# A hybrid attention layer on one core: a shorter lead, POOL's products moved to DVE, and the FFN's first groups in another order

## What is computed

```
h    = rmsnorm(x, pre_mix_norm)
proj = h @ w_in                                  # 1024 x 3072
rq, rk, rv, rg, mq, mk, mv = split(proj)
ret  = silu(rg) * head_rmsnorm(retention(rotary(rq), rotary(rk) / 8, rv))     # 4 heads
moba = causal softmax attention(mq, mk, mv) with a T5 bucket bias             # 8 heads of 64
mix  = concat([ret, moba]) @ w_out
x    = x + rmsnorm(mix, post_mix_norm)
h    = rmsnorm(x, pre_ffn_norm)
f    = (silu(h @ w_gate) * (h @ w_up)) @ w_down
x    = x + rmsnorm(f, post_ffn_norm)
```

## Time and profile before

| | |
|---|---|
| median of 3 timed runs | 317.04 us (316.82 to 317.07) |
| profiled execution | 318.91 us, its span 317.1 us |
| PE busy | 305.3 us (96%) |
| DVE, ACT, POOL busy | 182.7, 153.3, 27.6 us |
| granted PE clock | 0.998 of full speed |
| read from memory | 57.10 MB, 183 GB/s over the span |

### The profile page before, as it was taken

How to read it: one execution, slowest core, us unless ns; L and a number is a source line. 1 busy time by engine, 2 the same in 40 slices (tenths; PEclk the granted TensorE clock), 3 DMA queues, 4 the chain that set the end, 5 groups by cost and what they waited for, 6 DMA issues and landing times.

```text
span 317.1 us, 4124 instructions
## 1 busy us (share of the span) xinstructions
PE 305.3 (96%) x1432; PEld 248.8 (78%) x1432; DVE 182.7 (58%) x255; ACT 153.3 (48%) x254; POOL 27.6 (9%) x31
## 2 busy tenths in 40 slices
PE   7999987999999999999999999999999999999992
PEld 3788866888888888768888888888888888888881
DVE  2858265697467487899555555544444454551426
ACT  4889626446608174676444444444433333340322
POOL 4021056000002000540000000000000000000001
PEclk9999999999999999999999999999999999999999
DMA  6999974314541543169965555555566565400003
GB/s 216 398 407 373 413 308 134 134 66 153 180 144 57 198 156 111 66 231 317 367 203 179 179 190 180 168 184 191 198 198 198 198 196 183 149 0 0 0 2 132
DMA packets 17517, 58.35 MB, mean 184 GB/s; under 512 B 1997, under 2 KB 2517, under 8 KB 17504
## 3 DMA queue, kind: packets, MB, share of 16 engines
q1 hardware_dynamic: 17136, 57.06, 51.6%
q0 software_dynamic: 368, 1.11, 1.0%
HBM read 57.10 MB, written 1.06 MB: 183 GB/s over the span
## 4 chain that ended last, share of the span: by engine, by line
PE 85%; DVE 7%; ACT 3%; DMA 2%; POOL 2%; issue 1%; SPq 0%; DVEq 0%
PE bank L951 25%; PE bank L953 24%; PE bank L952 24%; PE bank L961 4%; DVE w_lo L681 2%; DMA raw<-in_w_in 2%; PE bank L978 1%; POOL xs L437 1%; PE bank L982 1%; PE bank L986 1%; ACT w_hi L451 1%; DVE d_lo L876 1%; ACT kz L518 1%; PE bank L1049 1%; DVE res L942 1%
## 5 line engine op out<-in xcount | busy, mean ns | idle before, releaser
L951 PE MATMUL bank<-w_hi,a_hi 128*128 128x512 f32 x256 | 101.9, 398 | 0.0
L953 PE MATMUL bank<-w_hi,a_lo 128*128 128x512 f32 x256 | 100.1, 391 | 0.0
L952 PE MATMUL bank<-w_lo,a_hi 128*128 128x512 f32 x256 | 99.6, 389 | 0.0
L617 ACT ACTIVATE sil<-bank,rstd 128x256 f32<-128x256 f32 x22 | 10.4, 473 | 96.1 <-PE bank L953 93.7
L953 PEld LDWEIGHTS bank<-w_hi,a_lo 128*128 128x128 f32 x256 | 48.0, 188 | 10.6
L952 PEld LDWEIGHTS bank<-w_lo,a_hi 128*128 128x128 f32 x256 | 48.2, 188 | 9.8
L951 PEld LDWEIGHTS bank<-w_hi,a_hi 128*128 128x128 f32 x256 | 48.1, 188 | 9.4
L869 DVE TENSOR_TENSOR w_lo<-raw,w_hi 128x1024 fp32r<-128x1024 f32 x40 | 49.6, 1276 | 6.7 <-ACT w_hi L602 6.7
L681 DVE TENSOR_TENSOR w_lo<-raw,w_hi 128x1024 fp32r<-128x1024 f32 x32 | 42.2, 1345 | 19.4 <-ACT w_hi L451 19.4
L884 DVE SCALAR_TENSOR_TENSOR hid<-bank,rstd,sil 128x256 f32<-128x256 f32 x22 | 10.7, 485 | 73.9 <-ACT sil L617 73.9
L602 ACT ACTIVATE w_hi<-raw 128x1024 fp32r<-128x1024 f32 x40 | 40.5, 1057 | 0.5 <-DMA raw<-in_w_gu 0.5
(11 more groups left out here) (119 smaller groups left out, 307.5 us busy)
## 6 DMA issues: line engine op xcount, KB each, us to landing
raw<-in_w_gu SPq DMA_DIRECT2D x44, 512.0 KB, 4.3
raw<-in_w_dn SPq DMA_DIRECT2D x22, 512.0 KB, 4.6
raw<-in_w_in SPq DMA_DIRECT2D x20, 512.0 KB, 8.5
raw<-in_w_out SPq DMA_DIRECT2D x8, 512.0 KB, 3.2
raw<-in_w_in SPq DMA_DIRECT2D x8, 256.0 KB, 5.8
xs<-in_x SPq DMA_DIRECT2D x2, 512.0 KB, 8.6
bias<-bias_row POOLq DMA_DIRECT2D x1, 1024.0 KB, 10.2
out<-res SPq DMA_DIRECT2D x4, 256.0 KB, 2.0
```

The lines of the kernel that those rows point to most:

```text
L617: act.activation(sil[:, t, :], pg[:, t, 0:FG], ACT.Silu, scale=rstd[:, X1_, t:t + 1]).then_inc(sil_ready[t], 1)
L951: pe.matmul(acc, hi, wh, start=first, stop=False)
L952: pe.matmul(acc, hi, wl, start=False, stop=False)
L953: return pe.matmul(acc, lo, wh, start=False, stop=last)
```

## The change

- LEAD is 4. ACT's evacuations of q, k and v stand ahead of the `w_hi` of their round. `LO_UNITS`, which says which `w_lo` DVE does in rounds 16 to 19, is shifted by one unit.
- The warm-up matmuls read a constant tile of ones; DVE's memset is gone. The bias row product stands behind the first block of unit 0; ACT issues the DMAs of its inputs, before its first table load.
- K's heads with odd numbers are copied out of PSUM by DVE, before the `w_lo` of unit 13, instead of by ACT.
- The three 128x1024 products of POOL are done by DVE: two in round 22, one behind the `w_lo` of `w_out`. POOL's memsets of `rqz` no longer wait for them. The residual of tile 1 goes to DVE as well; that of tile 0 stays.
- In the FFN each group does both tiles of gate and up first, then the down product of the group before for tile 0, then turns both tiles of `hid`, then the down product for tile 1. Group 0 and 1 are apart: group 1's gate and up go to bank45, and group 0's `hid` is turned, into bank01, in the middle of group 1's second tile. ACT and DVE have their queues rearranged to match.

```diff
-LEAD = 5
-LO_UNITS = {16: [], 17: [21], 18: [22], 19: [23, 24]}
+LEAD = 4
+LO_UNITS = {16: [], 17: [20], 18: [21], 19: [22, 23]}
...
-        pg = bank01
-        pt = bank45
+        def pg(g):
+            return bank45 if isinstance(g, int) and g == 1 else bank01
+        def pt(g):
+            return bank01 if isinstance(g, int) and g == 0 else bank45
...
-            pool.dma_start(rel[0:BUCKETS, :], rel_bias).then_inc(rel_loaded, 16)
-            pool.dma_start(bucket[:, :], bucket_c).then_inc(rel_loaded, 16)
...
-            for t in range(NT):
-                pool.wait_ge(x_loaded[t], 16)
-                pool.tensor_tensor(xg[:, t, :], xs[:, t, :], gp[:, :], ALU.mult).then_inc(xg_ready, 1)
-            pool.wait_ge(xg_ready, NT)
-            pool.tensor_tensor(gp[:, :], gm[:, :], gp[:, :], ALU.mult).then_inc(xg_ready, 1)
             pool.wait_ge(k_turned, NT)
-            pool.wait_ge(xg_ready, NT + 1)
+            pool.wait_ge(rstd_ready, NT)
...
+            act.dma_start(bucket[:, :], bucket_c).then_inc(rel_loaded, 16)
+            act.dma_start(rel[0:BUCKETS, :], rel_bias).then_inc(rel_loaded, 16)
...
+                if u == 3 * UPG:
+                    rows_out(v, 2, r_x, v_nat)
                 hi_in(u + LEAD)
...
             def group(g, g0, more=True):
+                if g0 > 1:
+                    h_hi_part(g - 1, 1)
+                ahead = 1 if g0 == 1 else GU - 1
                 if more:
-                    for s in range(GU - 1):
+                    for s in range(ahead):
                         hi_gu(g + 1, s, g0 + 1)
                 silu(g, 0)
-                h_hi_part(g - 1, 1)
+                if g0 == 1:
+                    for t in range(NT):
+                        h_hi_part(0, t)
                 if more:
-                    hi_gu(g + 1, GU - 1, g0 + 1)
+                    for s in range(ahead, GU):
+                        hi_gu(g + 1, s, g0 + 1)
+                silu(g, 1)
                 for j in range(DN):
                     hi_dn(g, j, g0)
-                silu(g, 1)
                 h_hi_part(g, 0)
...
-            dve.memset(junk[:, 0:CW // 2], 0.0).then_inc(zeros_ready, 1)
...
+                if u == K_T:
+                    for t in range(NT):
+                        dve.wait_ge(k_turned, t + 1)
+                        dve.tensor_copy(kz[64:P, 1:MH:2, t * P:(t + 1) * P],
+                                        wk[64:P, t, :].rearrange("p (b i) -> p b i", i=P)
+                                        ).then_inc(kT_odd, 1)
...
+                if u == MIX_T:
+                    dve.wait_ge(gp_loaded, 16)
+                    for t in range(NT):
+                        dve.wait_ge(x_loaded[t], 16)
+                        dve.tensor_tensor(xg[:, t, :], xs[:, t, :], gp[:, :], ALU.mult
+                                          ).then_inc(xg_ready, 1)
...
-            zeros = junk[:, 0:CW // 2].bitcast(BF16)
-            pe.wait_ge(zeros_ready, 1)
+            ones = nc.const_aps.tensor(1.0, (P, CW), BF16)
             for _ in range(WARM):
-                pe.matmul(bank67[:, 0, :], zeros[:, 0:P], zeros[:, 0:CW], start=True, stop=True)
+                pe.matmul(bank67[:, 0, :], ones[:, 0:P], ones, start=True, stop=True)
...
+                    if k == 0:
+                        bias_row_product()
...
+            def first_hidden(s):
+                if s == 1:
+                    for t in range(NT):
+                        turn_hidden(0, t)
+
             def group(g, g0):
-                gate_up(g, 0, g0)
-                turn_hidden(g - 1, 1)
+                for t in range(NT):
+                    gate_up(g, t, g0, hook=first_hidden if g0 == 1 and t == 1 else None)
                 down(g - 1, 0, g0 - 1)
-                gate_up(g, 1, g0)
-                turn_hidden(g, 0)
+                for t in range(NT):
+                    turn_hidden(g, t)
                 down(g - 1, 1, g0 - 1)
```

More of the change, by code:

```diff
@@ L237, in hybrid_layer @@
         mixn_ready = sem("mixn_ready")
-        x1_ready = sem("x1_ready")
+        x1_ready = [sem(f"x1_ready{t}") for t in range(NT)]
         gu_done = sem("gu_done")
@@ L431, in _ @@
                     factor(FACTORS.index((what, t)))
-            for t in range(NT):
[L434 to L438, removed]
+            for c in range(2):
+                cols = slice(c * CW, (c + 1) * CW)
+                pool.wait_ge(mixn_ready, c + 1)
+                pool.tensor_tensor(xs[:, 0, cols], xs[:, 0, cols], mix[:, 0, cols], ALU.add
+                                   ).then_inc(x1_ready[0], 1)
+            for t in range(NT):
                 factor(FACTORS.index((X1_, t)))
@@ L515, in _ @@
                         act.wait_ge(k_turned, t + 1)
[L516 to L520, removed]
+                        act.activation(kz[0:64, 0:MH:2, t * P:(t + 1) * P],
+                                       wk[0:64, t, :].rearrange("p (b i) -> p b i", i=P), ACT.Copy
+                                       ).then_inc(kT_ready, 1)
+                if u == UPG:
+                    act.wait_ge(nq_ready, 1)
+                    wait_factor(act, X_, NT - 1)
+                    rows_out(qn, 0, lambda t: nq[:, t:t + 1], q_nat)
+                if u == 2 * UPG:
+                    rows_out(kn, 1, r_x, k_nat)
+                if u == 3 * UPG:
+                    rows_out(v, 2, r_x, v_nat)
                 hi_in(u + LEAD)
@@ L646, in _ @@
             hi_gu(1, 2, 1)
+            hi_gu(1, 3, 1)
             wait_factor(act, X1_, 0)
             silu(0, 0)
-            hi_gu(1, 3, 1)
             x1_squares(1)
-            hi_dn(0, 0, 0)
             wait_factor(act, X1_, 1)
             silu(0, 1)
-            h_hi_part(0, 0)
-            hi_dn(0, 1, 0)
+            for j in range(DN):
+                hi_dn(0, j, 0)
             group(1, 1)
@@ L883, in hidden @@
                     dve.wait_ge(h_turned[t], g)
-                dve.scalar_tensor_tensor(out=hid[:, t, :], in0=pg[:, t, FG:2 * FG],
+                dve.scalar_tensor_tensor(out=hid[:, t, :], in0=pg(g)[:, t, FG:2 * FG],
                                          scalar=rstd[:, X1_, t:t + 1], in1=sil[:, t, :],
@@ L1020, in _ @@
                     ins.then_inc(w_used, 1)
-                if u == 1:
-                    pe.wait_ge(rel_one, 1)
-                    pe.wait_ge(rel_loaded, 32)
-                    pe.matmul(wk[0:MH, 0, 0:REV], rel[:, :], bucket[:, :], start=True, stop=True
-                              ).then_inc(brow_done, 1)
                 if u == Q_T:
@@ L1143, in gate_up @@
             def gate_up(g, t, g0, hook=None):
-                if not (isinstance(g, int) and g == 0):
+                if not (isinstance(g, int) and g <= 1):
                     pe.wait_ge(hid_ready[t], g)
@@ L1169, in turn_hidden @@
                     pe.wait_ge(hlo_ready[t], g)
-                turn(pt[:, t, :], hid[:, t, :], DN, h_turned[t])
+                turn(pt(g)[:, t, :], hid[:, t, :], DN, h_turned[t])
             def down(g, t, g0, last=False):
```

72 lines of the change are left out of this document (36 added, 36 removed).

## The result

The changed kernel took **312.81 us** (median of 4 timed runs, 312.37 to 312.85), the kernel before 316.96 in the same comparison (316.82 to 317.07): ratio 0.9866, 95% interval 0.9849 to 0.9883, so 4.15 us less. The forecast was 313.0. Its total is right, but the terms behind it aren't: one was about half as large in the timed runs as forecast, two were larger.

What follows compares the result with a forecast made beforehand. PE's own work plus the holes in it was taken to bound the kernel. Terms -0.74 - 2.93 - 0.81 - 0.2 + 0.7 = -4.0 us, off the median 317.04, gave 313.0 us; range 312.0 to 315.0.

Steps and rivals of the forecast that it cites:

- 1 to 4, start and K: From the warm-up to K's copies: only the bias row product's move gains, 0.74 us; the other parts cost or gain 0.
- 5, products: Block attention: with POOL's three products on DVE, both PE waits on the logits go, 2.93 us.
- 6, first FFN groups: FFN groups 0 and 1: waits of 0.81 and 0.2 us go, a new one of 0.7 us comes.
- 7, loop and end: Loop over the FFN groups: hid is ready within the 2.76 us of down product in between; cost 0.
- Warm-up on the constant: Kernel start: warm-up begins about 0.3 us earlier, but the second block still waits for data; worth 0.
- Bias row: Unit 0: the bias row product fits into 1.0 us where PE stood empty; gain 0.74 us.
- LEAD 4: Units 5 and 6: w_lo still arrive in time, with margins of 0.5 and 0.7 us; cost 0.
- K on DVE: Before unit 13's w_lo: two copies of 0.6 us each on DVE, done before the scores of head 0.
- the new wait: PE on group 1's hid of tile 1: 0.7 us taken; as a rival, 1.5 to 3 us, chance 0.13.
- the slower rival: FFN loop: hid over 2.76 us late makes PE wait in 10 groups; 319.0 at 0.6 us each, chance 0.05.
- no unit starves: Rival at the first units: w_lo come late with less lead; 314.5 at 2 us of lateness, chance 0.14.
- The third rival: Block attention: logits, Exp, w_hi and w_lo still deliver late, 1.5 to 2 of 2.93 us lost; 314.8, chance 0.06.

Runs made afterwards that it cites:

- e9: The changed kernel with the FFN part of the kernel before; products on DVE, start and middle as changed: 314.46 us, ratio 0.9898.
- e1: The kernel before with only the three POOL products moved to DVE and POOL's memsets of rqz right after the turn of k: 315.41 us, ratio 0.9942.
- e11: The changed kernel with the bias row product behind unit 1 again, ACT still issuing bucket: 313.33 us, ratio 0.9869.
- e10: The changed kernel with bucket and rel issued by POOL again, bias row product still inside unit 0: 312.51 us, ratio 0.9843.
- e4: The kernel before with each of POOL's three products released by the same event as a w_lo of DVE: 315.37 us, ratio 0.9945.
- e7: The changed kernel with group 1's silu and hid of tile 1 ahead of the last w_hi and w_lo of group 2: 312.28 us, ratio 0.9844.
- e6: The changed kernel with the two turns of hid of a group apart again from group 2 on: 312.76 us, ratio 0.9865.
- e5: The kernel before with each of POOL's three products released by the end of a w_lo: 315.25 us, ratio 0.9936.
- e0: The kernel before, unchanged, profiled a second time: 319.28 us, span 317.5.
- e8: e4 with a DVE memset of 512 spare columns before each of the three w_lo: 315.47 us, ratio 0.9919.

## Why the prediction was right, step by step

The mechanisms were right. The total came out to 0.2 us by luck: in the timed runs the products gave 1.4 us less than forecast, and the start and the FFN together 1.55 more.

| step | forecast | trace | timed runs |
|---|---|---|---|
| 1 to 4, start and K | -0.74 | -1.20 | -0.95 (e9 - e1) |
| 5, products | -2.93 | -3.46 | -1.55 (e1) |
| 6, first FFN groups | -0.31 | -1.14 | |
| 7, loop and end | 0 | -0.82 | 6 and 7: -1.65 (e9) |
| sum | -4.0 | -6.6 | -4.15 |

1. *Warm-up on the constant.* It starts at 0.78. The first real product is even later, 5.32 against 5.08 by the trace, since it waits for its activations. Worth 0, as forecast.
2. *Bias row.* It moved into the hole as forecast, and e11 prices that at 0.5 to 0.8 us. The term was forecast for a late second block; the second half of the first weight unit came to ACT at 5.45 instead of 6.69, and e10 shows that this goes with the queue that issues `bucket` and `rel`. The forecast moved those issues and counted only their own landing, not what they keep back.
3. *LEAD 4.* No unit starves. The `w_lo` of unit 5 ends at 19.6, PE wants it at about 20: the margin is 0.4, forecast 0.5.
4. *K on DVE.* 0.65 us a copy (0.6 taken), logits 1 and 2 at 42.9 and 47.83 (43.7 and 48.8 to 49.0 forecast). POOL's memsets cost the `w_lo` beside them nothing: by the rule of the Trainium skill that the forecast weighed, this trace (0.24 us in common) and that of e4 (0.93) agree.
5. *The products: the step that was mis-sized.* "Both waits go: 2.93 us." They went, but the term is the loss of one execution of the slower kind, in which POOL had come 0.31 us before `w_lo`. It was then subtracted from the median of executions that were 1.9 us faster than the profiled one. The forecast saw that gap and carried the difference over unchanged. That an execution is that much above the median says that some stall in it isn't typical, and the stall that hangs on a landing time was the one to suspect.
6. *The FFN's first groups.* The place and cause of the new wait were right, its size was 0.40 us (start to start, e7) against 0.7 taken. The waits that went cost more than their rows. The earlier trace rows shows 0.81 us, but the last matmul before it started at 134.14 and the turn at 135.33: 1.19 us, where 0.23 is the undisturbed distance, so 0.96 lost; for `d_lo` it is 0.33 against a row of 0.17. That gives -0.96 - 0.33 + 0.40 = -0.89 of the -1.14. The last 0.25 I can't assign to single instructions; the kernel after has fewer changes between kinds of product here.
7. *The loop.* No wait on `hid`, so the slower rival fell. "Cost 0" missed a gain of 0.058 us a group (e6), 0.5 us in nine groups, and 0.3 us behind them, where the kernel before still had a single turn and the late first product behind it (from the last group to the last matmul 5.18 us instead of 5.47, with the period taken off).

Rival by rival: no unit starves, the new wait isn't large, and the logits' ring delivers in time (e1, e5). The third rival said that 1.5 to 2 of the 2.93 us would be missing; 1.4 are missing in the timed runs, but not by its mechanism.

## What to carry to other kernels

Before a term from a profile is subtracted from a timed median, compare the profiled execution with that median, and ask which stall hangs on the landing time of a DMA: it may be there in some executions only, and then the timed runs fall into groups. A median of few runs doesn't show them: the first four of before all lay in the lower one. Where two engines exclude each other, the critical one needn't lose its turn; releasing the other one by the event that releases the critical one (e4), or by its end (e5), gave the whole gain without moving work (e4, e5). Count a stall by the distance of matmul starts, less the undisturbed distance, not by its idle row (0.96 for 0.81, 0.40 for 0.19).

## What the runs showed of the hardware

- A DVE operation with two inputs in SBUF and a POOL product exclude each other in both directions. First POOL by 0.08 us: DVE 3.39 us instead of 1.23 (e0). First DVE by 0.14 us: POOL 3.33 instead of 2.40 (e4).
- With a DVE memset of 128x512 f32 right before `w_lo`, a POOL product that started 0.40 to 0.44 us before `w_lo` was held off until its end (e8, at all three places: 3.79, 3.83, 3.83 us). I had not expected that, and by which operation it was held isn't shown. POOL memsets beside a `w_lo` cost neither anything (e4: 1.09 and 1.23 us, 0.93 in common).
- Two small loads issued by POOL at 1.3 and 2.0 us go with a second half of the first weight unit that comes to ACT some 1.4 us later than with ACT's issue (6.5 to 7.3 against 5.0 to 6.0 us; e10 changes nothing else). Why is open.
